# Expert layer of a decoder step: looking up expert rows against streaming both expert tables

## The chip, the cores and the metric
One core of a Trainium2 chip runs the whole program. The metric is the device time of one launch in microseconds (us), less is better. Everything is float32.

## The reference, cut to what matters
The layer is a mixer (projections, a gated chunk MLP, dilated window attention, output projection) and then the expert layer (PEER), for 512 prompt tokens and 32 sample tokens of width 1024. The change is in the expert layer alone:

```python
q = (xb @ w_q).reshape(TOK_BLK, PEER_HEADS, 2, DK_HALF)          # 8 heads, 2 halves of 128
s = einsum('thcd,hcnd->thcn', q, sub_keys)                       # 128 keys for each half
s1, i1 = top_k(s[:, :, 0], 16);  s2, i2 = top_k(s[:, :, 1], 16)
cand = s1[..., :, None] + s2[..., None, :]                       # 256 sums
top_s, pos = top_k(cand, 16)
eid = (i1 * 128 + i2) at pos                                     # one of 16384 experts
g = softmax(top_s)
hid = gelu(einsum('thkd,td->thk', u_tab[eid], xb))
y = einsum('thk,thkd->td', g * hid, v_tab[eid])                  # 8 heads x 16 experts a token
```

u_tab and v_tab have 16384 rows of 1024 floats, 64 MiB each. A token uses 128 of the rows of each. The result is added to the token, and a last RMSNorm gives the output.

## The kernel before, in words
The tokens lie in five tiles: 0 to 3 of 128 prompt tokens, and tile 4 of the 32 sample tokens. The host passes both tables side by side as `uv_tab`, so that row e holds u and v of expert e (8 KB). Each engine has its own program, written out in order, and they meet at semaphores.

The mixer goes through tile 0 first, then the others. Tile 0 is ahead in the expert layer too: its expert numbers are found early, GpSimd gathers its 128 u rows a token slot by slot (`gather_u`), and VectorE takes their dot products (`dots_to`, L1694) beside the projections and the attention of the other tiles. For the second half of tile 0, `gather_v` brings the 128 v rows of one token (512 KB) at a time into a ring of 12 buffers, and TensorE multiplies them by that token's weights (`weigh`, L896), in bursts of four tokens that `weigh_first` puts between parts of the output projections (`project_out`, L798) and the query jobs.

A query job (`JOBS`, L408 on) is one head for all tokens of tiles 1 to 4: two halves of 8 matmuls with 416 columns (`half_queries`, L851), then 2 small matmuls for each tile against the keys (`key_scores`, L871). ScalarE copies queries and scores out. Three of the eight jobs run ahead of the slots (`JOBS_AHEAD`), the other five between the slots of tile 1 (`job_part`).

From the scores VectorE finds the 16 experts of a head and tile (`route`, L1535): twelve links (`LINKS`), each of which waits for the one before, spread over other work by `go_on`.

Tiles 1 to 3 then take 128 slots each (a slot is one of 8 heads x 16 experts), tile 4 takes 32 with four groups of 32 partitions. For each slot:
- GpSimd, `gather_both` (L1896, issued at L1873): one indirect DMA brings the row of u and v of 128 experts, one for each token of the tile, 1 MB, into one of 6 buffers (`x_ring`). It waits for `x_free` (or `x_added`) of the slot six before.
- VectorE, `dot` (L1698): u times x, summed, one number a token.
- ScalarE, `weigh_slot` (L1248): Gelu of it, times the gate, and a 128x128 diagonal matrix `diag` of the result (three activations, of which the last two have line L1003).
- TensorE, `add_slot` (L901, matmuls at L907): diagonal times v, two matmuls with 512 columns, added up in PSUM (`acc`). For 20 slots of tile 1 VectorE does this in its place (`BY_DVE`, `add_rows`, L1711).

In order: tiles 1, 2, 3 and the samples. After each tile ScalarE reads the sum and squares it, VectorE scales it (`finish_y`), SyncE stores it.

Of the kernel before, what the change touches and what calls it, by code (L numbers as in the profile page):

```python
# [14 lines left out]
P = 128  # L15
D = 1024
# [31 lines left out]
NKEYS = 128  # L48
TOPK = 16
SLOTS = HEADS * TOPK  # L50
UR, VR, XR = 6, 12, 6
DG = 4
# [5 lines left out]
STEPS = [HEADS] * (NT - 1) + [HEADS // GROUPS]  # L58
FIRST = [sum(STEPS[:t]) for t in range(NT)]
NSTEP = sum(STEPS)  # L60

# [3 lines left out]
ROUTE_STEP = {g: [g + 2] for g in range(8, 24)} | {g: [2 * g - 22, 2 * g - 21] for g in range(24, 31)}  # L65
TOPS_ATT, EID_SAMPLE = 15, 5

JOBS_AHEAD = 3

def build(nc, x_p, x_s, k_cache, v_cache, gains, gain_cols, w_in, ln_gb, w_sT, b_sT, w_out, w_q, keysT, uv_tab,
# [3 lines left out]
    with ctx:  # L75
# [14 lines left out]
        def cut(area, a, *dims):  # L90
# [4 lines left out]
            if len(dims) == 3:  # L95
# [27 lines left out]
        x_ring = ([cut(area_r, s * 2 * D, 2 * D) for s in range(XR // 2)]  # L123
                  + [cut(area_r, 2 * PAIRS * TOK + s * 2 * D, 2 * D) for s in range(XR // 2)])
# [30 lines left out]
        y_junk = cut(area_v, NT * D, D)  # L155
# [17 lines left out]
        diag = [cut(area_c, s * P, P) for s in range(DG)]  # L173
# [3 lines left out]
        den = cut(area_v, (NT + 1) * D, NSTEP)  # L177
# [12 lines left out]
        tops = tops_all[:].rearrange("p (h k) -> p h k", h=HEADS)  # L190
# [28 lines left out]
        def wide(i, n):  # L219
            return bank[i].rearrange("p a b -> p (a b)")[:, 0:n]  # L220

        acc = bank[0]
        x_cur = wide(1, D)

# [31 lines left out]
        x_free, hid_ready, bent_ready, col_ready, diag_ready = (sem("x_free"), sem("hid_ready"), sem("bent_ready"),  # L256
                                                                sem("col_ready"), sem("diag_ready"))
        head_exped, head_gated, summed_den = sem("head_exped"), sem("head_gated"), sem("summed_den")
        eye_ready, numbered = sem("eye_ready"), sem("numbered")
        x_added, rest_added = sem("x_added"), sem("rest_added")  # L260
# [3 lines left out]
        samp_gates = sem("samp_gates")  # L264
# [78 lines left out]
        U_OF = [SLOTS] * (NT - 1) + [SLOTS // GROUPS]  # L343
        U_END = [sum(U_OF[:t + 1]) for t in range(NT)]
        V_OF = [n for _, n in TILES]

        X_END = [U_END[t] - U_END[0] for t in range(NT)]

        def x_slot(i):  # L350
            return (i + 1) % XR

        BY_DVE = [h * TOPK + j for h in range(HEADS - JOBS_AHEAD) for j in (4, 5, 9, 10)]

        def by_pe(i):
            return i - sum(d < i for d in BY_DVE)

        def tile_of(i):
            return next(t for t in range(NT) if i < U_END[t])  # L360

        N_ITER = NG - NG0 + 3
# [24 lines left out]
        def job_part(j):  # L388
            i, p = HEADS + JOBS_AHEAD + j // TOPK, {3: 0, 8: 1, 13: 2}.get(j % TOPK)
            return (i, p) if p is not None and i < len(JOBS) else None  # L390

# [14 lines left out]
        def sum_of(t):  # L406
            n = TILES[t][1]
            return x_tile[t][0:n, :] if t < SAMP else acc[0:n].rearrange("p a b -> p (a b)")  # L408
# [11 lines left out]
        def _(sp):  # L420
# [94 lines left out]
            sp.wait_ge(g_turned, NT)  # L515
            sp.wait_ge(roped, len(QK))
# [19 lines left out]
            for t in range(1, NT):  # L536
                load_x(t)
            for i in range(HEADS + 3, len(JOBS)):
# [4 lines left out]
            for t, (a, n) in enumerate(TILES):  # L543
                sp.wait_ge(y_ready, t + 1)
                if t < SAMP:
                    sp.dma_start(y_p[a:a + n, :], x_tile[t][0:n, :]).then_inc(y_out, 16)
                else:
                    sp.dma_start(y_s, x_tile[t][0:n, :]).then_inc(y_out, 16)
            sp.wait_ge(y_out, 16 * NT)
# [4 lines left out]
        def _(pe):  # L554
# [229 lines left out]
            def project_out(t, c, tokens=0):  # L784
# [9 lines left out]
                for k in range(KD):  # L794
                    if k == KD // 2:
                        weigh_first(tokens)
# [12 lines left out]
                weigh_first(tokens)  # L809
# [26 lines left out]
            def queries(i, tokens=0):  # L836
                for c in range(2):
                    half_queries(i, c, tokens)

            def half_queries(i, c, tokens=0):  # L840
# [9 lines left out]
                for k in range(KD):  # L850
                    mm = pe.matmul(half(4 + c)[:, 0:n], w[:, k, c * P:(c + 1) * P], featT[:, k, a:a + n],  # L851
                                   start=(k == 0), stop=(k == KD - 1))
                    if k == KD - 1:
                        mm.then_inc(q_done[c], 1)
                    if k % 4 == 3:
                        weigh_first(tokens)
# [25 lines left out]
            def start_sum(t):  # L882
                n = TILES[t][1]
                if t >= 2:
                    pe.wait_ge(acc_read, t)
                for c in range(2):
                    mm = pe.matmul(acc[0:n, c, :], ident[0:n, 0:n], x_tile[t][0:n, c * 512:(c + 1) * 512],
                                   start=(t != 1), stop=False, skip_group_check=True)
                return mm

            def weigh(j):
                s, c, g = j % VR, j // GROUPS, j % GROUPS
                pe.wait_ge(v_landed[s], 16 * (j // VR + 1))
                for e in range(2):
                    mm = pe.matmul(acc[CG * g:CG * g + CG, e, :], wd[g][:, c * CG:c * CG + CG],  # L896
# [4 lines left out]
            def add_slot(t, j):  # L901
                i = X_END[t - 1] + j
                s, n = x_slot(i), TILES[t][1]
                pe.wait_ge(x_landed[s], 16 * (i // XR + 1))
                pe.wait_ge(diag_ready, by_pe(i) + 1)
                for c in range(2):
                    mm = pe.matmul(acc[0:n, c, :], diag[by_pe(i) % DG][:, 0:n], x_ring[s][:, D + c * 512:D + (c + 1) * 512],  # L907
                                   start=(i == 0), stop=False, skip_group_check=True)
                mm.then_inc(x_free, 1)
# [19 lines left out]
            queries(0)  # L929
# [36 lines left out]
            project_out(1, 1, 4)  # L966
            for t in range(2, NT + 1):
                if t < NT:
                    project_out(t, 0, 4)
                    project_out(t, 1, 4)  # L970
# [4 lines left out]
            queries(HEADS, 4)  # L975
            for i in range(HEADS + 1, HEADS + JOBS_AHEAD):
                queries(i, 4)
                key_scores(i - 1)
            key_scores(HEADS + JOBS_AHEAD - 1)
            weigh_first(V_OF[0] - made[0])  # L980
            for t in range(1, NT):

                if t > 1:
                    start_sum(t)
                else:
                    pe.wait_ge(acc_read, 1)
                for j in range(U_OF[t]):
                    if X_END[t - 1] + j not in BY_DVE:
                        add_slot(t, j)
                    if t == 1 and job_part(j):  # L990
                        i, p = job_part(j)
                        if p < 2:
                            half_queries(i, p)
                        else:
                            key_scores(i)
                if t == 1:
                    pe.wait_ge(x_added, len(BY_DVE))
                    start_sum(1).then_inc(rest_added, 1)

        @block.scalar  # L1000
        def _(act):
# [223 lines left out]
            def exp_tops(t):  # L1225
                n = TILES[t][1]
                act.wait_ge(route_link, (t + 1) * HEADS * LINKS)
                nc.scalar.activation(tops[0:n], tops[0:n], ACT.Exp).then_inc(tops_exped, 1)

            def exp_head(k):  # L1230
                h = k % HEADS
                act.wait_ge(route_link, (k + 1) * LINKS)
                nc.scalar.activation(tops[:, h, :], tops[:, h, :], ACT.Exp,
                                     accum_out=den[:, k - HEADS:k - HEADS + 1]).then_inc(head_exped, 1)
# [13 lines left out]
            def weigh_slot(t, j):  # L1248
                i = X_END[t - 1] + j
                eye = ident[:] if t < SAMP else eye_samp  # L1250
                g = gate[:, j:j + 1] if t < SAMP else gate_grp[:, j:j + 1]
                act.wait_ge(hid_ready, i + 1)
                nc.scalar.activation(bent[:, j:j + 1], hid[t % 2][:, j:j + 1], ACT.Gelu).then_inc(bent_ready, 1)  # L1253
                if t < SAMP and j % TOPK == 0:
                    act.wait_ge(head_gated, FIRST[t] - HEADS + j // TOPK + 1)
                if t == SAMP and j == 0:
                    act.wait_ge(samp_gates, 1)
                act.wait_ge(bent_ready, i + 1)
                copy(w_col[:, j:j + 1], g, bent[:, j:j + 1]).then_inc(col_ready, 1)
                if i in BY_DVE:  # L1260
                    return
                if by_pe(i) >= DG:
                    act.wait_ge(x_free, by_pe(i) - DG + 1)
                act.wait_ge(col_ready, i + 1)
                copy(diag[by_pe(i) % DG][:, 0:TILES[t][1]], eye, w_col[:, j:j + 1]).then_inc(diag_ready, 1)

            def read_sum(t):
                n = TILES[t][1]
                if t == 0:
                    act.wait_ge(v_free, VR + V_OF[0])  # L1270
# [724 lines left out]
```

## Time and profile before

| | us |
|---|---|
| median of 3 runs | 1687.59 |
| lowest and highest | 1683.56, 1921.37 |
| the profiled execution, from its first to its last instruction | 1709.3 |

The profiled execution has no time of its own beside this span. A profile shows for each engine the instructions with start and length. PE is TensorE's matmuls, PEld its weight loads, DVE VectorE, ACT ScalarE, POOL GpSimd, SP SyncE.
### The profile page before, as it was taken

What the parts mean: (1) busy time and instruction counts of PE and PEld (TensorE: products, weight loads), DVE (VectorE), ACT (ScalarE), POOL (GpSimd) and SP (SyncE); (2) the same over time, 40 slices, a digit from 0 to 9 for tenths busy, and PEclk for the clock granted to TensorE, in tenths of its full rate; (3) what the DMA queues carried; (4) which work ended last, traced back from release to release, by engine and by line L of the source; (5) the groups of instructions that cost most, each with busy time, mean ns of one, the idle gap of its engine ahead of it and who ended that gap; (6) DMA issues with size and microseconds to landing.
All of it is one profiled execution on the core that took longest, in us unless ns stands there. A gap on an engine that the chain in (4) does not pass through costs nothing.

```text
span 1709.3 us, 17753 instructions
## 1 busy us (share of the span) xinstructions
PE 1404.9 (82%) x5164; PEld 622.7 (36%) x5164; DVE 1085.5 (64%) x2884; ACT 634.5 (37%) x1889; POOL 652.7 (38%) x703
## 2 busy tenths in 40 slices
PE   8999996768997978888878887777777777777786
PEld 5585663435333434334423232222223222222211
DVE  2459978868000046777766766666668888888654
ACT  2421113445211024344444454444445444444443
POOL 3034333322565653333333333333333333333332
PEclk9999996888998989999999999999999999999999
DMA  9798889999999999999999999999999999999997
GB/s 344 292 357 313 318 318 364 398 411 385 358 362 338 386 375 399 413 409 417 410 423 421 406 416 422 421 421 403 407 422 396 414 422 420 405 419 413 409 406 324
DMA packets 112144, 664.81 MB, mean 389 GB/s; under 512 B 13072, under 2 KB 14336, under 8 KB 52400
## 3 DMA queue, kind: packets, MB, share of 16 engines
q0 software_dynamic: 97824, 571.75, 83.4%
q1 hardware_dynamic: 14224, 91.93, 13.8%
q8 instruction: 42, 0.69, 0.2%
q14 instruction: 54, 0.44, 0.1%
HBM read 658.03 MB, written 5.60 MB: 388 GB/s over the span
## 4 chain that ended last, share of the span: by engine, by line
DMA 37%; PE 37%; issue 8%; ACT 7%; DVE 6%; another core or an unknown queue 3%; POOL 0%; ACTq 0%; SPq 0%; DVEq 0%; POOLq 0%
DMA area_r<-in_uv_tab,eid 36%; PE bank L907 11%; PE bank L627 9%; PE bank L851 4%; PE bank L896 4%; ACT area_c L1003 3%; PE bank L798 2%; DVE area_r L1703 2%; PE bank L558 1%; PE bank L871 1%; ACT L1253 1%; DVE area_x L1711 1%; DMA area_w<-in_w_in 1%; PE bank L767 1%
## 5 line engine op out<-in xcount | busy, mean ns | idle before, releaser
L907 PE MATMUL bank<-area_r,area_c 128*128 128x512 f32 (+1 forms) x1584 | 778.8, 624 | 213.8 <-ACT area_c L1003 212.8
L1873 POOL DMA_INDIRECT area_r<-in_uv_tab,eid x544 | 515.7, 948 | 944.0 <-PE bank L907 590.0
L1703 DVE CUSTOM_DVE_ANT_0 area_r<-area_r,bank 128x1024 f32<-128x1024 f32 x416 | 506.3, 1218 | 288.0 <-DMA area_r<-in_uv_tab,eid 287.3
L907 PEld LDWEIGHTS bank<-area_r,area_c 128*128 128x128 f32 (+1 forms) x1584 | 273.3, 188 | 713.0 <-issue 712.6
L1253 ACT ACTIVATE area_c<-hid 128x1 f32<-128x1 f32 x416 | 84.2, 202 | 538.8 <-DVE hid L1703 538.3
L1694 DVE CUSTOM_DVE_ANT_0 area_r<-area_r,bank 128x1024 f32<-128x1024 f32 x128 | 152.9, 1212 | 25.5 <-DMA area_r<-in_uv_tab,eid 22.7
L627 PE MATMUL bank<-area_w,area_t 128*128 128x384 f32 (+1 forms) x448 | 157.6, 509 | 4.1 <-DMA area_w<-in_w_in 3.5
L1003 ACT ACTIVATE area_c<-ident,area_c 128x128 f32<-128x128 f32 x364 | 146.1, 401 | 34.9 <-ACT area_c L1003 1.1
L1873 POOL DMA_INDIRECT area_r<-in_uv_tab,eidT x128 | 121.4, 948 | 82.0 <-issue 29.3
L1003 ACT ACTIVATE area_x<-bank 128x384 f32<-128x384 f32 (+8 forms) x123 | 49.9, 423 | 212.4 <-remote 59.4
L851 PE MATMUL bank<-area_t,area_w 128*128 128x416 f32 (+1 forms) x448 | 118.8, 418 | 6.1 <-issue 5.2
L1003 ACT ACTIVATE area_c<-gate,area_c 128x1 f32<-128x1 f32 x384 | 113.0, 294 | 13.9
L627 PEld LDWEIGHTS bank<-area_w,area_t 128*128 128x128 f32 x448 | 84.4, 192 | 68.0 <-issue 18.3
L851 PEld LDWEIGHTS bank<-area_t,area_w 128*128 128x128 f32 x448 | 70.4, 192 | 55.4 <-issue 54.1
L1397 DVE RECIPROCAL small<-small 128x1 f32<-128x1 f32 (+1 forms) x9 | 1.4, 158 | 113.3 <-issue 58.3
L896 PE MATMUL bank<-area_r,area_c 128*32 128x512 f32 x384 | 71.7, 633 | 0.9 <-issue 0.9
L1547 DVE MAX8 rt<-area_w 128x8 f32<-128x128 f32 (+1 forms) x80 | 19.3, 281 | 72.6 <-issue 52.0
L896 PE MATMUL bank<-area_r,area_v 128*32 128x512 f32 x128 | 64.4, 629 | 0.0
L798 PE MATMUL bank<-area_w,area_t 128*128 128x512 f32 x96 | 46.5, 631 | 1.7 <-issue 0.9
L1003 ACT ACTIVATE area_t<-bank 64x8 f32<-64x8 f32 (+5 forms) x111 | 28.6, 265 | 51.5 <-PE bank L558 28.3
L1487 DVE CUSTOM_DVE_ANT_0 area_x<-bank,area_c 128x256 f32<-128x256 f32 (+4 forms) x52 | 26.0, 535 | 23.9 <-PE bank L665 11.5
L1088 ACT ACTIVATE area_x<-area_x,att 128x256 f32<-128x256 f32 (+3 forms) x44 | 28.7, 653 | 31.2 <-DVE att L1487 19.1
(200 smaller groups left out, 1202.6 us busy)
## 6 DMA issues: line engine op xcount, KB each, us to landing
area_w<-in_w_in SPq DMA_DIRECT2D x12, 1536.0 KB, 11.1
area_w<-in_k_cache SPq DMA_DIRECT2D x8, 1920.0 KB
area_w<-in_w_q SPq DMA_DIRECT2D x14, 1024.0 KB, 6.8
area_r<-in_uv_tab,eid POOLq DMA_INDIRECT x544
area_w<-in_w_out SPq DMA_DIRECT2D x4, 2048.0 KB, 11.6
area_w<-in_v_cache SPq DMA_DIRECT2D x4, 1920.0 KB
area_v<-in_v_cache SPq DMA_DIRECT2D x4, 1152.0 KB
area_x<-in_x_p SPq DMA_DIRECT2D x6, 512.0 KB
```

Of the source, the lines that this page charges most:

```text
L627: mm = pe.matmul(out_half(u)[0:n, 0:w], featT[:, k, a:a + n], w_now[:, k, 0:w], start=(k == 0), stop=(k == KD - 1))
L798: mm = pe.matmul(ps[0:n, :], featT[:, k, a:a + n], w(k, c * 512, (c + 1) * 512), start=(k == 0), stop=False)
L851: mm = pe.matmul(half(4 + c)[:, 0:n], w[:, k, c * P:(c + 1) * P], featT[:, k, a:a + n], start=(k == 0), stop=(k == KD - 1))
L896: mm = pe.matmul(acc[CG * g:CG * g + CG, e, :], wd[g][:, c * CG:c * CG + CG], v_ring[s][:, e * 512:(e + 1) * 512], start=False, stop=False ...
L907: mm = pe.matmul(acc[0:n, c, :], diag[by_pe(i) % DG][:, 0:n], x_ring[s][:, D + c * 512:D + (c + 1) * 512], start=(i == 0), stop=False, ski ...
L1003: return nc.scalar.activation(out, src, ACT.Copy, scale=scale)
L1088: nc.scalar.activation(score_of(u)[0:r, 0:n], score_of(u)[0:r, 0:n], ACT.Exp, bias=st[0:r, 0:1], scale=-1.0, accum_out=st[0:r, 2:3]).then_ ...
L1253: nc.scalar.activation(bent[:, j:j + 1], hid[t % 2][:, j:j + 1], ACT.Gelu).then_inc(bent_ready, 1)
L1487: return vec.tensor_tensor_reduce(out=out, in0=scores, in1=counts, scale=-1.0, scalar=3e38, op0=ALU.add, op1=ALU.min, accum_out=least)
L1694: vec.tensor_tensor_reduce(out=u_ring[s], in0=u_ring[s], in1=x_cur, scale=1.0, scalar=0.0, op0=ALU.mult, op1=ALU.add, accum_out=hid[0][:, ...
L1703: vec.tensor_tensor_reduce(out=u, in0=u, in1=x_cur, scale=1.0, scalar=0.0, op0=ALU.mult, op1=ALU.add, accum_out=hid[t % 2][:, j:j + 1]).th ...
L1873: nc.gpsimd.indirect_dma_start(out=ring[s], out_offset=None, in_=table, in_offset=bass.IndirectOffsetOnAxis(ap=where, axis=0)).then_inc(la ...
```

## The change
Tile 0 and the samples still gather rows. Tiles 1 to 3 (384 tokens) don't. For them all 16384 experts are computed, in 128 blocks of 128 experts (`NBLK`):
- Pass 1, for each block b: `hidden(b)` multiplies the block of the u table (given by the host in transposed blocks, `u_blocks`, 512 KB) with the 384 tokens: 8 matmuls with 384 columns. ScalarE takes the Gelu out of PSUM (`gelu_block`) and stores four blocks at a time to a DRAM scratch, `h_scratch` (768 KB).
- Between these, for four tokens at a time (96 builds, one in each of the blocks 17 to 112), the matrix of gates by expert: VectorE makes one-hot matrices of the two key indices, one of them times the gate (`make_hots`), TensorE multiplies them, 4 matmuls with 128 columns (`build_weights`), ScalarE copies the result into one stage (`read_built`) and stores it every 8 builds (2 MB) to `w_scratch`. Before it writes that stage again, it waits for the store.
- Pass 2, for each block b: VectorE multiplies hidden by gates (`weigh_block`, 384 columns), TensorE multiplies the product with the v block (512 KB): 3 tiles x 2 matmuls with 512 columns (`add_block`).
- All eight query jobs run ahead of pass 1, five of them with a burst of four tile-0 tokens behind; 64 of tile 0's 128 tokens are weighed in pass 1 instead (16 bursts). The v ring has 8 buffers.
- The 32 sample slots go beside pass 2, one every 3 blocks, dot and sum on VectorE; 2 buffers.
- `route` ends in `picked`, the two key indices as numbers, for tiles 1 to 3.

```diff
+            def hidden(b):
+                pe.wait_ge(u_in[b % NU], 16 * (b // NU + 1))
+                if b >= 2:
+                    pe.wait_ge(gelued, b - 1)
+                for k in range(KD):
+                    mm = pe.matmul(half(4 + b % 2)[:, 0:ND], u_blk[b % NU][:, k * P:(k + 1) * P], featT[:, k, P:P + ND],
+                                   start=(k == 0), stop=(k == KD - 1))
+                mm.then_inc(h_done, 1)
...
+            def build_weights(w):
+                pe.wait_ge(hots_ready, w + 1)
+                out = build_half(build_at["weights", w])
+                for q in range(BUILT):
+                    mm = pe.matmul(out[:, q * P:(q + 1) * P], hot_second[w % 2][:, q, :], hot_first[w % 2][:, q, :],
+                                   start=True, stop=True)
+                mm.then_inc(built, 1)
...
+            def add_block(b):
+                pe.wait_ge(v_in[b % NV], 16 * (b // NV + 1))
+                pe.wait_ge(a_ready, b + 1)
+                for t in DENSE:
+                    for c in range(2):
+                        mm = pe.matmul(sums[t][:, c, :], a_blk[b % NA][:, (t - 1) * P:t * P], v_blk[b % NV][:, c * 512:(c + 1) * 512],
+                                       start=False, stop=(b == NBLK - 1), skip_group_check=True)
...
+            for i in range(HEADS, len(JOBS)):
+                half_queries(i, 0)
+                if i > HEADS:
+                    key_scores(i - 1)
+                half_queries(i, 1)
+                if i < HEADS + ROWS_QUERY:
+                    weigh_first(4)
...
+            for b in range(NBLK):
+                hidden(b)
+                if b in ROWS_AT:
+                    weigh_first(4)
+                for t in DENSE:
+                    if b == TURN_IDX[t]:
+                        turn_picked(t)
+                if 0 <= b - BUILD_FROM < NBUILD:
+                    build_weights(b - BUILD_FROM)
...
+            for t in DENSE:
+                start_sum(t)
+            for b in range(NBLK):
+                add_block(b)
+                if b == SAMPLE_SUM_AT:
+                    sum_samples()
...
+            def read_built(w):
+                if w % PER_BATCH == 0 and w > 0:
+                    act.wait_ge(w_stored, 16 * (w // PER_BATCH))
+                act.wait_ge(built, w + 1)
+                r, k = build_at["weights", w], w % PER_BATCH * BUILT
+                copy(w_out_stage[:, :, k:k + BUILT],
+                     half(BUILD_HALF[r % len(BUILD_HALF)]).rearrange("p (q i) -> p i q", q=BUILT)).then_inc(build_read, 1)
...
+            def make_hots(w):
...
+                vec.tensor_tensor(hot_second[s], numbers.unsqueeze(1).to_broadcast(across),
+                                  second[:, k:k + BUILT].unsqueeze(2).to_broadcast(across), ALU.is_equal)
+                for q in range(BUILT):
+                    ins = vec.tensor_scalar(hot_first[s][:, q, :], numbers, first[:, k + q:k + q + 1], gates[:, k + q:k + q + 1],
+                                            ALU.is_equal, ALU.mult)
+                ins.then_inc(hots_ready, 1)
+
+            def weigh_block(b):
...
+                vec.tensor_tensor(out, w_load[b // WQN % 2][:, :, b % WQN, :], hid_in, ALU.mult).then_inc(a_ready, 1)
...
+            go_on(links[2], 4)
+            finish_gates(DENSE[0])
+            go_on(links[2], 6)
+            for w in range(NBUILD):
+                t = DENSE[w // PER_TILE]
+                k = w % PER_TILE
+                if k == PER_TILE - 2 and t < DENSE[-1]:
+                    go_on(links[t + 1])
+                    finish_gates(t + 1)
+                make_hots(w)
+                go_on(links[t + 1], 4 if t < DENSE[-1] else 2)
```

## Rows read from the trace of the kernel before

**Rows 1.** The page's span, busy time, and the span in 40 slices
```profile
span 1709.3 us, 17753 instructions
...
PE 1404.9 (82%) x5164; PEld 622.7 (36%) x5164; DVE 1085.5 (64%) x2884; ACT 634.5 (37%) x1889; POOL 652.7 (38%) x703
...
DMA  9798889999999999999999999999999999999997
```

**Rows 2.** The chain of work that ended last, shares of the span
```profile
DMA 37%; PE 37%; issue 8%; ACT 7%; DVE 6%; another core or an unknown queue 3%; POOL 0%; ACTq 0%; SPq 0%; DVEq 0%; POOLq 0%
```

**Rows 3.** Stretches: length, busy of each engine, clock, DMA share, GB/s
```profile
441.00:552.00 111.00, 98.62 (x527) 38.20 (x525) 6.91 (x9) 16.48 (x37) 65.74 (x69) 0.94 0.95 344
631.00:850.00 219.00, 186.28 (x511) 84.80 (x504) 161.11 (x366) 95.52 (x285) 78.72 (x83) 0.98 0.99 403
850.00:1700.00 850.00, 665.17 (x1355) 231.29 (x1354) 601.03 (x1551) 366.32 (x1096) 312.66 (x332) 0.97 1.00 413
```

**Rows 4.** Groups by line: busy, mean ns, idle before and its releaser
```profile
L907 PE MATMUL bank<-area_r,area_c 128*128 128x512 f32 (+1 forms) x1584 | 778.8, 624 | 213.8 <-ACT area_c L1003 212.8
L1873 POOL DMA_INDIRECT area_r<-in_uv_tab,eid x544 | 515.7, 948 | 944.0 <-PE bank L907 590.0
L1703 DVE CUSTOM_DVE_ANT_0 area_r<-area_r,bank 128x1024 f32<-128x1024 f32 x416 | 506.3, 1218 | 288.0 <-DMA area_r<-in_uv_tab,eid 287.3
```

**Rows 5.** Timeline of TensorE, projections: start, length, what, records
```profile
244.12 15.75 PE L627 MATMUL bank<-area_w,area_t 128*128 128x384 f32 x48
259.80 1.93 PE L624 MATMUL bank<-area_w,area_t 128*32 128x128 f32 x45
```

**Rows 6.** Matmuls with 512 columns: a timeline row, and a group
```profile
1100.52 5.46 PE L907 MATMUL bank<-area_r,area_c 128*128 128x512 f32 x12 [2.00 <-ACT area_c L1003]
...
L627 PE MATMUL bank<-area_w,area_t 128*128 128x512 f32 x64 | 27.9, 593 | 0.6 <-issue 0.6
```

**Rows 7.** Timeline of TensorE, query jobs and bursts of tile 0
```profile
552.32 4.75 PE L851 MATMUL bank<-area_t,area_w 128*128 128x416 f32 x8 [3.81 <-issue]
561.87 0.64 PE L896 MATMUL bank<-area_r,area_c 128*32 128x512 f32 x3
563.74 3.06 PE L851 MATMUL bank<-area_t,area_w 128*128 128x416 f32 x8
819.87 5.75 PE L851 MATMUL bank<-area_t,area_w 128*128 128x416 f32 x16
825.46 1.88 PE L907 MATMUL bank<-area_r,area_c 128*128 128x512 f32 x4
```

**Rows 8.** Timeline of TensorE, matmuls with 128 columns
```profile
114.91 1.95 PE L851 MATMUL bank<-area_t,area_v 128*128 128x128 f32 x16
116.70 1.95 PE L851 MATMUL bank<-area_t,area_x 128*128 128x128 f32 x16
...
844.65 2.35 PE L871 MATMUL bank<-area_r,area_x 128*128 128x128 f32 x16
846.93 5.62 PE L907 MATMUL bank<-area_r,area_c 128*128 128x512 f32 x12
```

**Rows 9.** Tail: timeline from the last matmul on
```profile
1704.00 1.01 ACT L1282 ACTIVATE area_v<-bank 32x1024 f32<-32x1024 f32 x1 [0.54 <-PE bank L907]
1707.02 0.33 SPq L548 DMA_DIRECT2D out_y_s<-area_x  x1
```

**Rows 10.** One route on VectorE, first and last; two groups
```profile
596.95 0.49 DVE L1547 MAX8 rt<-area_w 128x8 f32<-128x128 f32 x2 [51.99 <-issue]
607.64 0.17 DVE L1609 SCALAR_TENSOR_TENSOR eid<-rt 128x16 uint32<-128x16 f32 x1 [0.15 <-DVE rt L1604]
...
L1506 DVE TENSOR_SCALAR area_r<-area_r,att 128x128 f32<-128x128 f32 x12 | 3.4, 287 | 0.4
...
L1595 DVE TENSOR_TENSOR area_w<-rtu,iota 128x512 f32<-128x512 uint32 x32 | 22.0, 687 | 1.5 <-DVE rtu L1590 0.8
```

**Rows 11.** ScalarE, one copy of 512 columns out of PSUM
```profile
505.62 0.60 ACT L1003 ACTIVATE area_x<-bank 128x512 f32<-128x512 f32 x1 [6.82 <-PE bank L806]
```

**Rows 12.** DMA issues: count, KB each, median us to landing
```profile
area_w<-in_w_out SPq DMA_DIRECT2D x4, 2048.0 KB, 11.6
out_y_p<-area_x SPq DMA_DIRECT2D x3, 512.0 KB, 7.6
```

More of the change, by code:

```diff
@@ L57 @@
 LINKS = 12
-STEPS = [HEADS] * (NT - 1) + [HEADS // GROUPS]
-FIRST = [sum(STEPS[:t]) for t in range(NT)]
-NSTEP = sum(STEPS)
+NBLK = N_EXPERTS // P
+DENSE = range(1, NT - 1)
+ND = len(DENSE) * P
+NU, NV, NA = 4, 4, 3
+HQ, HLOADS = 4, 3
+TB, WQN = 32, 8
+BUILT = 4
+NBUILD = ND // BUILT
+PER_TILE = P // BUILT
+PER_BATCH = TB // BUILT
 DOTS_FIRST, DOTS_PROJ = 12, 75
@@ L171, in build @@
         wd = [cut(area_c, g * D, D) for g in range(3)] + [cut(area_v, (NT - 1) * D, D)]
-        diag = [cut(area_c, s * P, P) for s in range(DG)]
+        x_samp = cut(area_c, 0, D)
+        acc_samp = cut(area_c, 2 * D, D)
         eye_samp = cut(area_c, D, NSAMP)
@@ L548, in _ @@
                     sp.dma_start(y_s, x_tile[t][0:n, :]).then_inc(y_out, 16)
+            for i in range(NT):
+                store_y(i)
             sp.wait_ge(y_out, 16 * NT)
@@ L833, in turn_xn, with half_queries @@
                     mm.then_inc(xn_turned, 1)
[L836 to L840, printed above, removed]
+            def half_queries(i, c):
                 h = JOBS[i][0]
@@ new lines, in build_half, with turn_picked @@
+            def build_half(r):
+                if r >= len(BUILD_HALF):
+                    pe.wait_ge(build_read, r - len(BUILD_HALF) + 1)
+                return half(BUILD_HALF[r % len(BUILD_HALF)])
+            def turn_picked(t):
+                pe.wait_ge(tile_gated, t)
+                out = build_half(build_at["picked", t])
+                for i, src in enumerate((picked[t % 2][:, 0, :], picked[t % 2][:, 1, :], gate[:])):
+                    mm = turn(out[:, i * P:(i + 1) * P], src, P)
+                mm.then_inc(idx_turned, 1)
@@ L1383, in _ @@
+            store_hidden(NBLK // HQ - 1)
+            exp_tops(SAMP)
+            load_table(ACT.Sqrt)
+            square_y(0)
+            load_table(ACT.Gelu)
+            for j in range(SAMPLE_SLOTS):
+                weigh_slot(j)
+            load_table(ACT.Sqrt)
+            for i in range(1, NT):
+                square_y(i)
         @block.vector
@@ L1847, in _ @@
-            finish_y(SAMP)
+            dve.wait_ge(v_out, 16 * (NT + 1))
+            for h in range(HEADS):
+                go_on(route(HEADS * DENSE[0] + h))
+            links = {t: routings(range(HEADS * t, HEADS * (t + 1))) for t in range(DENSE[1], NT)}
+            go_on(links[2], 4)
[9 more added lines that the diff above has]
+                go_on(links[t + 1], 4 if t < DENSE[-1] else 2)
@@ new lines, in _ @@
+            go_on(links[SAMP])
+            set_x_samp()
+            sample_indices()
+            for b in range(NBLK):
+                weigh_block(b)
+                if b == 2:
+                    finish_gates(SAMP)
+                if b == 8:
+                    finish_y(0)
+                j, k = divmod(b - SAMPLE_FROM, SAMPLE_STEP)
+                if 0 <= j < SAMPLE_SLOTS:
+                    if k == 0:
+                        sample_dot(j)
+                    if k == 2:
+                        sample_add(j)
@@ L1849, in _ @@
+            for i in range(1, NT):
+                finish_y(i)
         @block.gpsimd
@@ L1945, in shape_tables @@
     rope = np.concatenate([c, c, -s, s], axis=1).astype(np.float32)
[L1946 removed]
+    iota = np.tile(np.arange(P, dtype=np.float32), (P, 1))
     tril = (r[:, None] <= r[None, :]).astype(np.float32)
```

494 lines of the change are left out of this document (253 added, 241 removed).

## The prediction

> **What bounds the kernel now.** I read the page's span and slices first: the DMA engines are at 9 or 10 tenths from the middle of the span to the end, while no engine is full [rows 1]. The chain that ended last is made of DMA and PE in equal parts, 37% each [rows 2]; that is an average over two kinds of stage, so I cut the span. From 850 to 1700 us, slots alone, DMA is at a share of 1.00 and 413 GB/s, PE is busy 665 of 850 us and VectorE 601 [rows 3]. 332 gathers of 1 MB go in 850 us: 2.56 us for one, and 1 MB at 413 GB/s is 2.5 us. The groups agree: VectorE's dot waits 287 us for its gathers, TensorE waits 213 us for ScalarE's diagonals, which come from that dot, and GpSimd waits 590 us for TensorE to free a buffer [rows 4]. So the ring is full of gathers under way, and the bytes set the pace. The 416 slots, from about 640 us to the last matmul at 1703.5 [rows 9], are a DMA stage.
>
> The change takes the bytes away there. So the question is only what TensorE costs in their place, and I price it record by record.
>
> **The new matmuls.** The longest stream of 384-column matmuls is 48 records from 244.12 to 259.80: 0.327 us a record [rows 5]. With 512 columns, 12 records over three slots take 5.46 us; less the last one's own 0.59 that is 0.443 from start to start; a group of 64 records is busy 27.9, so 0.436 each [rows 6]. For 128 columns there are two rows: 16 records in 1.79 us (0.112 each) and 16 in 2.28 (0.143) [rows 8].
>
> Pass 1: 128 blocks x 16 records x 0.327 = 669 us.
> Pass 2: 128 blocks x 12 records at 0.436 to 0.443, 5.23 to 5.31 a block; I take 5.26: 673 us.
> Builds: 96 x 8 records at 0.112 to 0.143, 0.90 to 1.14 a build; 1.02 taken: 98 us (range 86 to 109).
>
> These three alone are 1440 us of TensorE, more than the 1064 us of all slots (384 of the 416 are of the tiles concerned). TensorE becomes the bound, unless one of the terms is wrong by a third.
>
> **The path, step by step.**
> Up to the first query job at 552.3 [rows 7] the work is the same, but 7 bursts of tile 0 (28 tokens) are gone from the output projections (72 tokens before, 44 after). A burst of four tokens takes 563.74 - 561.87 = 1.87 us on TensorE [rows 7]. That gives 13 us back: 539. More isn't to be had, although DMA stands at 0.95 there [rows 3]: the bursts don't wait much in the rows, and 44 tokens are 22 MB. The two v buffers fewer hold up GpSimd only; the 8 left are 4 MB of lead, two bursts.
> Query jobs: a half is 16 records from 819.87 to 825.46, 5.59 us [rows 7], so 11.2 a job. The scores take 2.28 us when ScalarE keeps up [rows 8], and up to 4.6 if each tile waits for a copy of 0.6 [rows 11] behind 0.57 of matmuls; I take 2.8. Eight jobs x 14.0 = 112, and five bursts 9: 660. Five of these jobs stood between slots before, where DMA hid them; now nothing does. The waits in front of pass 1 (copies of the last queries and scores) add 2: pass 1 starts near 663.
> Pass 1: 669, plus 16 bursts x 1.87 = 30, builds 98, three turns of indices 2: 799, ends near 1462. With builds a block is 6.25, without 5.23.
> Pass 2: the start of three sums, 12 records, 5; 673; the samples' sum, 8 records, 4: 682, ends near 2144.
> Tail: before, 1704.0 - 0.54 to 1709.3 is 5.8 us with a 128 KB store at its end [rows 9]; now a tile of 512 KB is last, whose store lands in at most 7.6 us on a full DMA system [rows 12]. I take 8: 2152.
>
> **What lies beside it, at nothing.** DMA: a block of pass 1 moves 0.5 MB of u, 0.19 of hidden and 0.25 of gates, with a token every 1.5 blocks some 1.3 MB in 6.2 us, 210 GB/s against the 413 shown; pass 2 the same order with the samples' 1 MB every three blocks. Buffers are four blocks deep, some 20 us. ScalarE: Gelu of 384 and a copy of 512 columns, near 0.6 each [rows 11], 1.2 of 6.25. VectorE: a route is 596.95 to 607.81, 0.9 a link [rows 10]. Behind the builds of tiles 1 and 2 stand four links each, 3.6, and the one-hots, one 512-wide comparison 0.69 and four 128-wide ones at 0.29 [rows 10], 1.85: 5.5 against 6.25. That is hidden, but by 0.8 us only. Tile 1's routes keep up with the query jobs (10.9 against 14.0), end near 675, and its gates are wanted at block 14, 70 us later. The sample slots (32 x 2.5 = 80 us at the end before) go beside pass 2: VectorE has 0.5 for the product and 2.6 for a slot every third block, of 15.8.
>
> Against the median: the span is 21.7 above the median of the runs. If those belong to the slots' DMA, nothing of them is left in the new kernel; if to the mixer, all. The slots are 62% of the span, so I take off 7: 2145.
>
> **A rule weighed against the rows.** The price above holds for passes 0.32 to 0.44 apart, as the rows have them. The Trainium skill ("TensorE: Matmul & The Clock Gate", Back-to-back issue gap) gives a sustained spacing of about 131 ns a matmul for 512 columns and 81 for 128. The Trainium skill ("FP8 and Floating Point Precision") counts four passes for true float32. By the two, a 512-column float32 matmul would take an estimated 0.52 us where the rows have 0.87, and by a line between 81 and 131 a 384-column one 0.46 where they have 0.65; the two passes over the tables would be near 400 and 470 us, and the sum near 1680: no change at all. This is the rival "not slower" below in the skill's numbers; the trace disagrees in every long stream.
>
> **Rivals.**
> A, the stage of the gates. There is one buffer for 2 MB, and ScalarE stands in order before the copy behind each store; Gelu of the next block stands behind it. TensorE can go on for two blocks and three builds, 13.6 us. A 2 MB load takes 11.6 us [rows 12], 2 MB at 413 GB/s 5.1; four stores of 512 KB at 7.6 each [rows 12] would be 30. At 11.6 nothing is seen. At 30, 11 waits x 17 = 185 us: 2335. For it: stores of this size aren't in the trace, and reads come beside it. Against: DMA is half empty.
> B, VectorE sets the builds' pace. If the one-hots cost twice my value, a build is 7.4 against 6.25, on 44 builds (22 for each of two tiles with four links): +50, 2195; with links late besides, up to 80.
> C, the clock. Granted clock was 0.97 over the slots, where PE has gaps, and 0.94 at 441 to 552 [rows 3]. If it stays at 0.97 though TensorE has no gaps, 3% of 1440 us: +43, 2190. It is in my range.
> D, not slower: the matmuls run faster in long streams without slot waits than in the chunks I read. To reach 1709 the passes over the tables must give back 443 of 1342 us, that is 0.219 a record with 384 columns and 0.293 with 512. The rows have 48 in a row at 0.327, and 384 columns at 2.4 GHz and two cycles a column are 0.320. Against it speaks every stream; for it only that none in the trace lasts longer than 16 us. At 0.22 and 0.29 it gives 1700.
>
> **How the numbers follow.** Forecast 2145, chance 0.80, its own range 2100 to 2195: builds -12 to +11, 512 columns -4 to +6, scores -4 to +14, tail -3 to +3, the offset to the median -15 to +7, clock up to +43. A has 0.09, B 0.06, C in full and other waits (a late table block, a late gate) 0.03, D 0.02. The range for 8 in 10 goes from 2095 to 2260: below, the sum of the small terms; above, half of A, or B and C together. All but D are slower by far more than the 2% that a measurement of this kernel can tell from no change (34 us): slower 0.98, same 0.01, faster 0.01.
>
> **What would show it.** PE near 9 in every slice from 663 us on, starts of `hidden` 5.2 apart without and 6.2 with builds, of `add_block` 5.3. DMA at half its share. TensorE idle before `hidden` only for a microsecond or less; 5 us or more every eighth block, released by ScalarE, is A; idle before `build_weights` released by VectorE is B. Pass 1 ends near 1460, pass 2 near 2145. The prediction is wrong if records with 384 columns lie under 0.3 us apart, or if pass 1 is over 850 us.

## The result, and the profile after

| | us |
|---|---|
| changed kernel, median of 4 runs (lowest, highest) | 2093.1 (2087.8, 2095.7) |
| kernel before, median of the runs beside it | 1685.6 |
| ratio, with its 95% interval | 1.241 (1.238 to 1.244) |
| span of the profiled execution | 2091.8 |

Slower by 24%, as forecast in kind: 2145 was predicted, with 2095 as the low end. The measured time lies 52 us under the prediction and 2 us under the range. One of the four runs of the kernel before was in a slower state, at 1921 us, and the ratio goes by fast runs alone.

The page of the changed kernel, busy time and slices:

```profile
span 2091.8 us, 21597 instructions
...
PE 2029.6 (97%) x7945; PEld 1109.8 (53%) x7945; DVE 871.3 (42%) x2670; ACT 340.6 (16%) x860; POOL 292.2 (14%) x319
...
PE   8999968899999999999999999999999999999998
...
PEclk9999967999999999999999999999999999999999
DMA  9798999989533555565565544466566866777642
```

Against [rows 1]: TensorE went from 82% to 97%, and from the ninth slice on it stands at 9 tenths or more, but for the last; DMA, full to the end before, is busy little more than half of the time in the new stages. The chain of waits says the same, where PE and DMA had 37% each [rows 2]:

```profile
PE 89%; DMA 6%; DVE 2%; issue 2%; ACT 1%; POOL 0%; SPq 0%; DVEq 0%; ACTq 0%
PE bank L991 32%; PE bank L962 31%; PE bank L913 6%; PE bank L696 6%; PE bank L982 4%; DMA area_r<-in_uv_tab,eid 4%; PE bank L952 3%; PE bank L865 2%; PE bank L930 1%; PE bank L627 1%; PE bank L836 1%; DMA area_x<-in_x_p 1%; DMA area_w<-in_w_in 1%; DVE area_r L1802 1%; DMA w_scratch<-area_w 1%
```

L962 is `hidden`, L991 `add_block`, L982 the builds. Their groups, with the copy that stands behind the stores of gates (the last row):

```profile
L962 PE MATMUL bank<-area_t,area_r 128*128 128x384 f32 x2048 | 677.8, 486 | 0.9 <-issue 0.6
L991 PE MATMUL bank<-area_w 128*128 128x512 f32 x1536 | 659.6, 592 | 0.0
...
L982 PE MATMUL bank<-area_r 128*128 128x128 f32 x768 | 102.6, 276 | 0.0
...
L1109 ACT ACTIVATE area_w<-bank 128x512 f32<-128x512 f32 (+2 forms) x132 | 72.0, 546 | 197.2 <-DMA w_scratch<-area_w 95.5
```

TensorE stood still 0.9 us before the 2048 records of pass 1 and 0.0 before the others. Nothing else is left on the path there. The three stages, from the view of stretches (columns as in [rows 3]): pass 1, pass 2, query jobs:

```profile
636.13:1417.34 781.21, 780.93 (x3082) 482.30 (x3083) 357.04 (x1298) 129.28 (x241) 57.55 (x58) 1.00 0.55 195
1417.34:2085.60 668.26, 668.26 (x1557) 294.55 (x1555) 151.17 (x238) 28.00 (x85) 28.10 (x30) 1.00 0.63 217
515.75:636.13 120.38, 118.89 (x466) 65.32 (x465) 55.92 (x232) 19.82 (x49) 20.56 (x22) 1.00 0.44 157
```

And the steady state of pass 1 on TensorE's timeline, a block with its build:

```profile
742.57 5.33 PE L962 MATMUL bank<-area_t,area_r 128*128 128x384 f32 x16
747.74 1.05 PE L982 MATMUL bank<-area_r 128*128 128x128 f32 x8
748.63 5.33 PE L962 MATMUL bank<-area_t,area_r 128*128 128x384 f32 x16
```

A block takes 747.74 - 742.57 = 5.17 us, its build 748.63 - 747.74 = 0.89. (The second number of a row is a printed length; lengths overlap, so the cost is read from start to start.)

### The profile page after: what moved, and what is told of

Its sections match the earlier page's. It is cut to its first block, busy times and chain, and to the rows that moved or that the text cites. A ratio compares the mean times of both kernels' runs of the same rounds, so it can differ in the third digit from the quotient of the medians.

```text
span 2091.8 us, 21597 instructions
## 1 busy us (share of the span) xinstructions
PE 2029.6 (97%) x7945; PEld 1109.8 (53%) x7945; DVE 871.3 (42%) x2670; ACT 340.6 (16%) x860; POOL 292.2 (14%) x319
## 4 chain that ended last, share of the span: by engine, by line
PE 89%; DMA 6%; DVE 2%; issue 2%; ACT 1%; POOL 0%; SPq 0%; DVEq 0%; ACTq 0%
PE bank L991 32%; PE bank L962 31%; PE bank L913 6%; PE bank L696 6%; PE bank L982 4%; DMA area_r<-in_uv_tab,eid 4%; PE bank L952 3%; PE bank L865 2%; PE bank L930 1%; PE bank L627 1%; PE bank L836 1%; DMA area_x<-in_x_p 1%; DMA area_w<-in_w_in 1%; DVE area_r L1802 1%; DMA w_scratch<-area_w 1%
## 5 line engine op out<-in xcount | busy, mean ns | idle before, releaser
L962 PE MATMUL bank<-area_t,area_r 128*128 128x384 f32 x2048 | 677.8, 486 | 0.9 <-issue 0.6
L991 PE MATMUL bank<-area_w 128*128 128x512 f32 x1536 | 659.6, 592 | 0.0
L962 PEld LDWEIGHTS bank<-area_t,area_r 128*128 128x128 f32 x2048 | 381.4, 190 | 248.5 <-issue 4.0
L991 PEld LDWEIGHTS bank<-area_w 128*128 128x128 f32 x1536 | 291.8, 190 | 367.7 <-issue 367.7
L2013 POOL DMA_INDIRECT area_r<-in_uv_tab,eid x144 | 137.5, 955 | 824.8 <-DVE eid L1750 205.6
L1802 DVE CUSTOM_DVE_ANT_0 area_r<-area_r,bank 128x1024 f32<-128x1024 f32 x128 | 153.2, 1212 | 33.5 <-DMA area_r<-in_uv_tab,eid 33.2
L982 PEld LDWEIGHTS bank<-area_r 128*128 128x128 f32 x768 | 99.6, 191 | 32.4 <-issue 10.9
L1836 DVE TENSOR_SCALAR area_r<-area_v,area_w 128x128 f32<-128x128 f32 x384 | 106.4, 343 | 0.0
L1109 ACT ACTIVATE area_w<-bank 128x512 f32<-128x512 f32 (+2 forms) x132 | 72.0, 546 | 197.2 <-DMA w_scratch<-area_w 95.5
L982 PE MATMUL bank<-area_r 128*128 128x128 f32 x768 | 102.6, 276 | 0.0
L1378 ACT ACTIVATE area_c<-hid 128x1 f32<-128x1 f32 x32 | 6.5, 203 | 555.2 <-DVE hid L1810 555.2
```

The lines of the kernel that those rows point to most:

```text
L962: mm = pe.matmul(half(4 + b % 2)[:, 0:ND], u_blk[b % NU][:, k * P:(k + 1) * P], featT[:, k, P:P + ND], start=(k == 0), stop=(k == KD - 1))
L982: mm = pe.matmul(out[:, q * P:(q + 1) * P], hot_second[w % 2][:, q, :], hot_first[w % 2][:, q, :], start=True, stop=True)
L991: mm = pe.matmul(sums[t][:, c, :], a_blk[b % NA][:, (t - 1) * P:t * P], v_blk[b % NV][:, c * 512:(c + 1) * 512], start=False, stop=(b == N ...
L1109: return nc.scalar.activation(out, src, ACT.Copy, scale=scale)
L1802: vec.tensor_tensor_reduce(out=u_ring[s], in0=u_ring[s], in1=x_cur, scale=1.0, scalar=0.0, op0=ALU.mult, op1=ALU.add, accum_out=hid[0][:, ...
L1836: ins = vec.tensor_scalar(hot_first[s][:, q, :], numbers, first[:, k + q:k + q + 1], gates[:, k + q:k + q + 1], ALU.is_equal, ALU.mult)
```

## The experiments

**The kernel before, profiled again.** No edit.

> The kernel before, unchanged, for a second profile. The changed kernel reached its output projections 12.8 us earlier than the profile before (419.4 against 432.1 us), though nothing was changed up to there but the order of one small load. Theory 1, chance between executions: this profile has its first output projection matmul several us away from 432.1, nearer 420, and a span nearer the median of 1685.6 than 1709.3. Theory 2, the change speeds the mixer up: it comes at 432 again, within 3 us.

The span is 1682.3, in a single run. Its first output projection comes at 421.1 and its first query half at 528.4, 24 us ahead of the 552.3 of [rows 7]: 11 us by the start of the projections, 13 in the stage of projections itself. That stage in the first profile, then in this one:

```profile
432.12:552.32 120.20, 107.50 (x542) 42.10 (x542) 7.23 (x10) 22.08 (x43) 72.37 (x77) 0.92 0.95 349
421.12:528.41 107.29, 106.75 (x541) 42.09 (x541) 7.20 (x10) 21.95 (x43) 71.98 (x76) 0.99 1.01 386
```

TensorE stood still for 12.7 us in the first and 0.5 in the second, with the same work, and DMA moved 349 GB/s against 386. The experiment on half the bytes below, which leaves this stage as it is, takes 106.6 us for it. The start of the projections varies more: 417.5 us in the changed kernel and 420.9 to 430.5 in the profiles of the six edits. So theory 1 holds: the execution I forecast from was 27 us longer than this one, and all of it ahead of the slots. From first slot to last matmul it had 1064 us (639.7 to 1703.4), this one 1064 too (611.9 to 1676.3). Why that execution was slower there is not shown.

**Fewer tokens ahead of the queries, in the kernel before.**

```diff
-                    if k == KD // 2:
-                        weigh_first(tokens)
```

> Kernel before with one burst of four tile-0 tokens behind each output projection in place of two, so that 44 tokens and not 72 are weighed ahead of the queries, as in the changed kernel; the rest follow at the end of the query jobs. From the first output projection to the first query half was 120 us before and is 96 us in the changed kernel; the forecast had taken off 13 (7 bursts x 1.87). Theory 1, the stage was held up by the gathers of v rows, so a burst costs more than its matmuls: the stage shrinks to 96 to 100 here too. Theory 2, only the matmuls go: 107. Total time: within 10 us of the kernel before, since the same bytes are gathered and the slots start when the last token is weighed.

1704.2 us, ratio 1.010 (1.006 to 1.014): slower by 18, where I had said within 10. From the first projection to the first query half it is 86.8 us (426.3 to 513.1), against 107.3 in the second profile of the kernel before: 20 less, not 13. Theory 1 is nearer, but I had set its numbers by the first profile. In the changed kernel the same stretch is 98.3 (417.5 to 515.8), only 9 under 107.3, so it is 11 longer than here. TensorE waits 4.2 us of them for the load of a tile of tokens (`in_x_p`); in one edit of the changed kernel where it doesn't (twice the links, below) the stretch is 92.9. The rest of the 11 is not explained. The changed kernel's ring of v rows also has 8 buffers in place of 12 (the prediction says two fewer; it is four). With 6, in the float16 kernel below, the stretch is 111.3, and TensorE waits 6.3 us in it for gathers; but no run changes the ring alone.

What was gained in the projections is lost behind them. From the first query half to the first slot it takes 119.4 us (513.1 to 632.5) against 83.5 in the second profile of the kernel before (528.4 to 611.9): 36 more, where the seven bursts moved there are 13 us of TensorE. DMA moved 344 GB/s from 420 to 550 us here, against 390. So the gathers of v rows seem to be on the path before the slots too; the argument goes by these numbers, no run isolates it.

**Half the bytes for each slot, in the kernel before.**

```diff
-                gather(x_ring, x_slot(i), uv_tab, eid[:, a:a + 1], x_landed)
+                gather([x[:, 0:D] for x in x_ring], x_slot(i), single, eid[:, a:a + 1], x_landed)
```

The v rows of the slots are left out (the buffers' old contents are multiplied).

> Kernel before, but each slot of tiles 1 to 4 gathers 512 KB (one row of 4 KB for each token) in place of 1 MB; v rows of these slots stay what lies in the buffer, all instructions remain. Theory 1, bytes set the slots' pace (2.56 us for 1 MB): the DMA part falls to 1.28 and TensorE's 4 records a slot, 1.75 to 1.83 us, become the pace with some waits, 1.9 to 2.1 us a slot: 1450 to 1530 us. Theory 2, the chain of dot, gelu, diagonal and matmul sets it: less than 30 us are gained.

1480.7 us, ratio 0.877 (0.874 to 0.881). A slot takes 600 / 295 = 2.03 us:

```profile
800.00:1400.00 600.00, 537.75 (x1192) 218.16 (x1192) 534.59 (x1461) 322.50 (x966) 277.29 (x295) 0.99 0.80 260
```

As many rows are gathered as before, each half as long, so it was the bytes that set the pace, and TensorE and VectorE (90 and 89% busy here) stood half a microsecond behind.

**Half of the matmuls of pass 1, in the changed kernel.**

```diff
-                for k in range(KD):
+                for k in range(KD // 2):
```

Half of the sum over the width is left out in `hidden`; all loads stay.

> Changed kernel with 4 of the 8 matmuls of each block of pass 1 (half of the sum over the width is left out), all loads remain. Theory 1, TensorE's records set pass 1: 8 records of 0.323 less in each of 128 blocks, 330 us, of which blocks with four links of routing give back what VectorE needs more than TensorE: 5.5 to 5.9 us a build against 3.5, on 44 builds, some 90 to 105 us. So 1855 to 1870 us, blocks without builds at 2.6 us. Rival, pass 1 is held by loads or by the stage of the gates: less than 150 us are gained, and blocks without builds stay above 4 us.

1840.3 us: 253 less than 2093.1. Theory 1 holds: TensorE's records set pass 1. But 77 of the 330 us are given back, not 90 to 105, and the time came out under the stated 1855. Pass 1 takes 507 us (643.2 to 1150.4) against 781, so 56 are given back in it; 15 more are a wait for VectorE's first product at the start of pass 2, and the start of pass 1 lay 7 us later. In pass 1 it is not mainly VectorE that holds, which I had named for all of it:

```profile
799.55 1.05 PE L982 MATMUL bank<-area_r 128*128 128x128 f32 x8
800.45 2.75 PE L962 MATMUL bank<-area_t,area_r 128*128 128x384 f32 x8
803.03 1.05 PE L982 MATMUL bank<-area_r 128*128 128x128 f32 x8
803.92 2.75 PE L962 MATMUL bank<-area_t,area_r 128*128 128x384 f32 x8
806.50 1.05 PE L982 MATMUL bank<-area_r 128*128 128x128 f32 x8
813.81 4.77 PE L962 MATMUL bank<-area_t,area_r 128*128 128x384 f32 x8 [6.26 <-ACT area_v L1353]
```

Blocks with builds go at 3.47 us, and then TensorE waits 6.26 us for ScalarE's Gelu, which stands behind the store of the gates: rival A, as soon as the blocks are short. Of TensorE's waits in pass 1 26.5 us are of this kind, 8.0 are for VectorE's one-hots before the builds, 3.0 for loads of the u table. They are 38 of the 56 us. The other 18 are matmuls that ran slower: the block behind the wait in the last row has a length of 4.77 us where 2.75 is usual, at a granted clock of 0.57 (813.8 to 818.4), and over pass 1 the clock is 0.97 where the changed kernel has 1.00.

**Every stage of gates stored twice, in the changed kernel.**

```diff
-                nc.scalar.dma_start(w_scratch[m], ...).then_inc(w_stored, 16)
+                for dst in (w_second, w_scratch):
+                    nc.scalar.dma_start(dst[m], ...).then_inc(w_stored, 16)
```

> Changed kernel, but every stage of gates is stored twice, to two scratch tensors (2 MB and 2 MB), and the stage counts as free when both have landed. In the changed kernel ScalarE waited 8.7 us on average for one store (95.5 us in 11 waits), and TensorE did not stand still for it. Theory 1, TensorE has a reserve of two blocks and three builds, 2 x 5.16 + 3 x 0.89 = 13.0 us, and a pair takes 16 to 18: 3 to 5 us at each of 11 waits, 30 to 55 us, so 2123 to 2150. Theory 2, stores run side by side at no cost because the DMA engines are half empty: 2093 within 5.

2143.3 us, 50 more than 2093.1: theory 1. Pass 1 takes 828 us (641.9 to 1469.9) in place of 781. The waits, of TensorE and of ScalarE (us in total, times, the longest), and TensorE behind one of them, with the view of that stretch:

```profile
PE bank L963 <- ACT area_v L1354: 31.0, 11, 6.0
...
ACT area_w L1110 <- DMA w_scratch<-area_w: 160.2, 11, 17.4
...
919.28 7.98 PE L963 MATMUL bank<-area_t,area_r 128*128 128x384 f32 x16 [6.05 <-ACT area_v L1354]
927.10 1.05 PE L983 MATMUL bank<-area_r 128*128 128x128 f32 x8
...
919.28:927.10 7.82, 7.82 (x16) 4.35 (x17) 0.00 (x0) 1.22 (x3) 0.00 (x0) 0.67 0.00 0
```

The 47 us are two things. TensorE stands still 31.0 us, 2.8 at each of the 11 waits. The other 16 are matmuls at a lower clock behind them: the block above takes 7.82 us in place of 5.17, at a granted clock of 0.67, and TensorE is busy 797 us in this pass against 781 with the same records. I had the sum right, 3 to 5 us a time, but not this part of it. A pair is waited for 14.6 us on average, one store 8.7. By these means TensorE's reserve is 14.6 - 2.8, some 11.8 us (an estimate) and not 13.0, because ScalarE still has a copy and a Gelu to do when the store has landed. The longest wait for one store in the changed kernel is 11.6: TensorE waited 0.3 us for a Gelu once. Rival A was hidden, but by little.

**Twice the links behind each build, in the changed kernel.**

```diff
-                go_on(links[t + 1], 4 if t < DENSE[-1] else 2)
+                go_on(links[t + 1], 8 if t < DENSE[-1] else 2)
```

> Changed kernel, with 8 links of routing behind each build of tiles 1 and 2 in place of 4: no work is added, but VectorE has 7.2 + 1.8 = 9.0 us of it in each of 11 builds for each of two tiles, against TensorE's 6.05 for a block with its build. Theory 1, VectorE was hidden by little (5.4 of 6.05) and runs at most two builds ahead: 22 x 3 us, less some ahead, +50 to +65 us, 2143 to 2158. Theory 2, VectorE has slack that the rows don't show: within 10 us of 2093.

2110.0 us, 17 more; between the theories. Pass 1 takes 795 us (643.8 to 1438.9), 14 more than in the changed kernel; 11.9 us of them are ten waits of TensorE for the one-hots, at most 1.7 us each. I had said "less some ahead" without a number: two builds of lead are 12 us for each of the two tiles, and 22 x 3 less 24 is 42; the links, at 0.8 in place of 0.9, make 22 x 2.2 less 24, 24. So VectorE stood further from the path than I had it, and rival B with it.

**Float16 in both passes and the builds.** The matmuls of tile 0, queries and routing stay in float32; sums are in float32. ScalarE turns the loaded blocks into float16. Other things change with it: both scratch tensors hold float16, half the bytes; the stage of gates has two buffers; the v ring of tile 0 has 6 buffers and that of the u blocks 3; the samples' gathers start only behind pass 1.

```diff
-                    mm = pe.matmul(half(4 + b % 2)[:, 0:ND], u_blk[b % NU][:, k * P:(k + 1) * P], featT[:, k, P:P + ND],
+                    mm = pe.matmul(half(4 + b % 2)[:, 0:ND], u16[b % NU16][:, k * P:(k + 1) * P], featT16[:, k, :],
...
-                        mm = pe.matmul(sums[t][:, c, :], a_blk[b % NA][:, (t - 1) * P:t * P], v_blk[b % NV][:, c * 512:(c + 1) * 512],
+                        mm = pe.matmul(sums[t][:, c, :], a_blk[b % NA][:, (t - 1) * P:t * P], v16[b % NV16][:, c * 512:(c + 1) * 512],
...
+                copy(u16[b % NU16], u_blk[b % NU]).then_inc(u_cast, 1)
...
+                copy(v16[b % NV16], v_blk[b % NV]).then_inc(v_cast, 1)
...
-        w_out_stage = cut(area_w, 2 * PIECE, P, TB)
+        w_out_stage = [low(area_w, 2 * PIECE + s * P * TB // 2, P, TB) for s in range(2)]
```

> Changed kernel with the matmuls of both passes and of the builds in float16, summed in float32 as before. ScalarE turns each u and v block into float16 after its load (1.0 us a block), Gelu, one-hots and gates are written as float16, the two scratch tensors hold float16, the stage of gates has two buffers, the v ring of tile 0 six. Then others set the pace: VectorE's 5.4 us behind the 44 builds with four links (240), 3.6 behind the other 52 (190), ScalarE or DMA at 1.6 to 2 us in the 32 blocks without builds (60), and DMA in pass 2 with 126 MB at 413 GB/s (305). With 636 ahead of pass 1 and 6 behind: 1440 to 1480 us, below the kernel before. Rival, TensorE's cost does not lie in float32 but in weights and waits: above 1800 us.

1437.0 us, ratio to the kernel before 0.852 (0.848 to 0.856): faster than both kernels, and 656 us faster than the changed one. Blocks on TensorE's timeline:

```profile
800.76 1.46 PE L979 MATMUL bank<-area_r 128*128 128x384 f16 x8
802.06 0.39 PE L999 MATMUL bank<-area_r 128*128 128x128 f16 x4
802.29 1.46 PE L979 MATMUL bank<-area_r 128*128 128x384 f16 x8
...
814.46 2.74 PE L979 MATMUL bank<-area_r 128*128 128x384 f16 x8 [5.38 <-ACT area_r L1126]
```

1.30 us for what took 5.17, and 0.23 for 0.89: half the records, each half as long. The matmul's float32 was the cost of the change. The last row is a block behind a wait (ScalarE had no u block to turn, its load was late): its 8 records take 2.74 us, twice as long, and the granted clock there is 0.50 of the full one, which is the level of 1.2 GHz. That stretch, then pass 1 and pass 2:

```profile
814.40:817.20 2.80, 2.74 (x12) 1.11 (x16) 0.00 (x0) 2.16 (x5) 0.00 (x0) 0.50 1.02 413
...
656.18:1080.20 424.02, 283.93 (x1674) 135.93 (x1675) 342.71 (x1273) 247.77 (x368) 57.64 (x58) 0.84 0.82 287
...
1097.50:1426.00 328.50, 213.74 (x776) 79.07 (x776) 119.75 (x232) 146.11 (x193) 39.21 (x30) 0.82 0.99 364
```

In pass 1 VectorE is the busiest engine now, and TensorE waits 117.7 us for its one-hots; in pass 2 the DMA engines are full again, at 0.99. The total came out 3 us under my range, but its parts did not: pass 1 took 424 us where I had 490, pass 2 with its start 346 where I had 305, and the part before them 656 where I had 636. They partly cancel, so the total is near by luck. The 15% are also no comparison of like with like: the kernel before keeps float32, and what float16 would do for it wasn't tried; what float16 costs in accuracy isn't part of this document.

## Why the prediction was right and wrong, point by point

The mechanism was right. DMA set the slots' pace before (half the bytes: 12% off the time). TensorE's three terms stand in its place without a gap, at a clock of 1.00. What I counted at nothing was nothing: DMA at 0.55 and 0.63 of its share in the passes, VectorE behind the builds, ScalarE's wait for its store (95.5 us, 0.3 of it on TensorE), the samples beside pass 2.

What failed is the size of the terms. The sum was 60 us too high, every term on the same side:

| step | forecast | measured | difference |
|---|---|---|---|
| first query half | 539 | 515.8 | -23 |
| query jobs | 124 | 120.4 | -4 |
| pass 1 | 799 | 781.2 | -18 |
| pass 2 | 682 | 668.3 | -14 |
| tail | 8 | 6.2 | -2 |
| span | 2152 | 2091.8 | -60 |

**The largest single error is in "Against the median".** The span of the profile before was 21.7 us above the median, and I gave most of it to the slots' DMA, because the slots are 62% of the span, and took off 7. The second profile shows where it was: ahead of the slots, 24 us by the first query half, while the slots took 1064 us in both. All of it should have come off, since the changed kernel keeps that part: 2130 in place of 2145, 15 us. The changed kernel's own profile has no such offset (2091.8 beside 2093.1), though its stages ahead of pass 1 were 6 to 8 us quicker than in the three edits of it with float32 (636.1 against 641.9 to 643.8), so that much of the table's first line is chance. There was a sign in the rows: a clock of 0.94 and 344 GB/s in 441 to 552, with TensorE busy 98.6 of 111 us [rows 3]. I read them as a property of the stage, and wrote that the bursts don't wait much in the rows, where TensorE stands still for 12 us.

**The step that failed by more in total is "The new matmuls": the prices of records were high, by one to two per cent for the passes and 15% for a build.** For 384 columns I took 0.327 from the longest stream [rows 5]; it is 5.17 / 16 = 0.323. That stream is 0.18 us longer than 48 x 0.323, and its weight loads have a gap of 0.2 us. For 512 columns I took 5.26 a block; 668.3 us less 5 for the starts and 4 for the samples' sum are 659, 5.15 a block, 0.429 a record. The 5.46 us of [rows 6] hold a gap between two slots, and the weight loads in them (TensorE's, in the kernel before) show both it and the clean price:

```profile
1102.31 0.19 PEld L907 LDWEIGHTS bank<-area_r,area_c 128*128 128x128 f32 x1 [0.24 <-issue]
1102.74 0.19 PEld L907 LDWEIGHTS bank<-area_r,area_c 128*128 128x128 f32 x1 [0.24 <-issue]
1103.17 0.19 PEld L907 LDWEIGHTS bank<-area_r,area_c 128*128 128x128 f32 x1 [0.24 <-issue]
1103.99 0.30 PEld L907 LDWEIGHTS bank<-area_r,area_c 128*128 128x128 f32 x2 [0.63 <-issue]
```

They start 0.43 us apart, and once 0.82. A build is 0.89 (I took 1.02, the middle between a clean row and one with waits for ScalarE's copies [rows 8]). Over both passes and the builds these are 7, 14 and 12 us, 33 of the 52 by which the forecast was too high. The clean price of each kind was the right one, since in the new kernel nothing waits. (For the tail I read 7.6 us as the most that a store takes; in [rows 12] it is a median. It cost 2 us.)

The Trainium skill ("TensorE: Matmul & The Clock Gate", Back-to-back issue gap) has two prices, and I weighed only one of them. Its sustained figures, rival D in the skill's numbers, are contradicted again: a float16 matmul with 384 columns takes 1.30 / 8 = 0.163 us from start to start, not near the 0.115 of the line between its 81 and 131 ns (an estimate). Its other formula, columns / 2.4 GHz + 2.5 ns, which it calls the gap of isolated matmuls, gives 0.1625 for it, and the trace agrees. With two passes in each record of a float32 matmul (an estimate by that formula, 2 x 160 + 2.5) it gives 0.3225 for 384 columns and 0.4292 for 512, beside the 0.323 and 0.429 of this trace; both passes over the tables would have been within 2 us.

**The range.** 384 columns had no lower bound in it at all, although the prices of both passes were read from rows with a gap in them, so their errors had one sign. The low end of 2095 is not the sum of the small terms either, as the prediction says: with every low end (builds -12, 512 columns -4, scores -4, tail -3) and the whole offset of 22 the sum of 2152 ends near 2107. The missing term (-8) makes it 2099, and the clean price of 512 columns (5.15 and not 5.23 a block) 2089, which would have held the result.

**Rivals.** A is real but hidden: with some 12 us of reserve and 7.7 to 11.6 us of waiting it costs nothing, with a pair of stores 50 us, with short blocks up to 6 us a time. B needs twice the links to show, 14 to 17 us. C didn't occur in the changed kernel: busy without a gap, TensorE had a clock of 1.00. D fell with the steady state of both passes.

## What to carry to other kernels

Before trading gathered bytes for dense matmuls, price the matmuls in the data type they will have: here the float32 records of 128 blocks twice cost 1320 us where the bytes they saved had cost about 980 (384 slots of 2.56), and in float16 the same plan takes 15% less than the kernel before in float32. Forecast a stage without waits from distances between starts that hold no wait. And where the profile's span stands off the median, find the stage that holds the difference before it is shared out; a low clock and a low rate in one stage is where to look.

## What the runs showed of the hardware that I had not expected

- A float32 matmul leaves two records of 0.323 us for 384 columns and 0.429 for 512, where float16 leaves one of 0.163 for 384. So float16 was faster by 4.0 on TensorE. The prediction had no sum for it; the expectation of that run had.
- A wait of 5 or 6 us of TensorE cost more than its length. The block behind it ran at a lower granted clock: 7.82 us in place of 5.17 at 0.67, behind 6.05 us of standing still (stores twice); 2.74 in place of 1.46 at 0.50, behind 5.38 (float16). With the pair of stores this is 16 of 47 us, with half the matmuls 18 of 56. In the float16 kernel the clock is 0.84 and 0.82 over the two passes, TensorE busy 67 and 65% of the time between waits; what that costs in total was not tried.
- A 2 MB store is waited for 8.7 us on average (7.7 to 11.6), two issued together 14.6 (up to 17.4). DMA is busy 0.59 of the time over that pass, but while the longest pair is under way (901.2 to 918.5 us) its share is 0.93, at 379 GB/s: the mean of a stage did not show it.
- Weighing fewer tile-0 tokens ahead of the queries makes the kernel before slower by 18 us, although every engine has the same work. It fits that gathers that aren't issued while DMA has room are paid for later; that this is the cause is argued and not shown.
